# A hybrid decoder layer on one core: x enters transposed, split without the token norm, the norm's factor applied to the projections' results

## The reference

```
h    = x * rsqrt(mean(x*x) + 1e-6) * norm_g          # token norm: one factor per token, one gain per feature
proj = h @ w_in                                       # 1024 x 4608, split in ten parts
oa   = rmsnorm(retention(qa, ka, va), ret_norm_g)     # 4 heads of 128, chunks of 128 tokens, a state
ob   = rglru(conv4(xb))                               # 512 channels, gates by sigmoid, a scan over tokens
oc   = attention(rmsnorm(qc), rmsnorm(kc), vc)        # window of 128, ALiBi, sinks, 4 heads on 2 kv heads
y    = x + concat(oa*silu(ga), ob*silu(gb), oc*silu(gc)) @ w_out
```

## Time and profile before

| | |
|---|---|
| median of three runs | 729.69 us |
| the profiled execution: its span, which is its own time as shown | 730.9 us |
| TensorE matmuls busy | 718.1 us, 98% |
| VectorE, ACT, POOL busy | 296.6, 268.6, 100.3 us |
| mean granted clock of TensorE | 0.981 |
| loaded and stored | 50 MB, 68 GB/s in the mean |

### The profile page before, as it was taken

One profiled execution on the slowest core, in us unless ns is written; L12 is line 12 of the kernel. 1 busy time (PEld: TensorE's weight loads), 2 busy tenths in 40 slices (PEclk: granted clock), 3 DMA queues, 4 the chain that ended last, 5 costly groups with the idle time before them and its releaser, 6 DMA issues. The chain is left out here.

```text
span 730.9 us, 11478 instructions
## 1 busy us (share of the span) xinstructions
PE 718.1 (98%) x4486; PEld 662.0 (91%) x4486; DVE 296.6 (41%) x693; ACT 268.6 (37%) x693; POOL 100.3 (14%) x228
## 2 busy tenths in 40 slices
PE   6999999999999999999999999999999999999998
PEld 4999989999999899999999998999989988888884
DVE  5824421232424213788632386317733362211102
ACT  5822422231323222678923464326453351000000
POOL 2201600353525000000002211122100000000000
PEclk9999989999999899999999999999999999999999
DMA  7511042103030211110131011031011351222111
GB/s 247 188 59 58 1 158 74 59 2 119 1 119 1 90 34 54 58 39 21 59 125 55 18 59 30 1 95 49 12 30 58 144 202 31 84 87 86 58 37 36
DMA packets 22887, 50.04 MB, mean 68 GB/s; under 512 B 1645, under 2 KB 15341, under 8 KB 20498
## 3 DMA queue, kind: packets, MB, share of 16 engines
q1 hardware_dynamic: 22834, 49.31, 19.8%
HBM read 42.22 MB, written 9.12 MB: 70 GB/s over the span
## 5 line engine op out<-in xcount | busy, mean ns | idle before, releaser
L377 PE MATMUL proj<-big 128*128 128x352 f32 (+1 forms) x960 | 311.3, 324 | 0.6 <-ACT big L786 0.6
L378 PE MATMUL proj<-big 128*128 128x352 f32 (+1 forms) x960 | 298.4, 311 | 0.0
L379 PE MATMUL proj<-big 128*128 128x352 f32 (+1 forms) x960 | 298.4, 311 | 0.0
L377 PEld LDWEIGHTS proj<-big 128*128 128x128 f32 x960 | 185.8, 193 | 9.9 <-issue 6.7
L378 PEld LDWEIGHTS proj<-big 128*128 128x128 f32 x960 | 185.6, 193 | 0.7
L379 PEld LDWEIGHTS proj<-big 128*128 128x128 f32 x960 | 185.6, 193 | 0.0
L1108 DVE TENSOR_TENSOR big<-raw,big 128x512 fp32r<-128x512 f32 x72 | 49.5, 694 | 62.7 <-ACT big L772 62.7
L1515 POOL TENSOR_SCALAR stat<-stat 128x1 f32<-128x1 f32 (+3 forms) x77 | 15.6, 203 | 321.4 <-ACT junk L900 197.3
L379 PE MATMUL branch<-big,m_parts 128*128 128x512 f32 x144 | 56.0, 389 | 0.0
L378 PE MATMUL branch<-big,m_parts 128*128 128x512 f32 x144 | 56.0, 389 | 0.0
L377 PE MATMUL branch<-big,m_parts 128*128 128x512 f32 x144 | 56.0, 389 | 0.0
(11 more groups left out here) (213 smaller groups left out, 940.5 us busy)
## 6 DMA issues: line engine op xcount, KB each, us to landing
raw<-w_units SPq DMA_DIRECT2D x18, 1024.0 KB, 4.8
mixed<-x_prompt SPq DMA_DIRECT2D x8, 512.0 KB, 5.2
x_res<-x_prompt SPq DMA_DIRECT2D x8, 512.0 KB, 4.2
out_y_prompt<-y_out SPq DMA_DIRECT2D x8, 512.0 KB, 2.9
raw<-w_out SPq DMA_DIRECT2D x6, 512.0 KB, 3.9
y_out<-w_out SPq DMA_DIRECT2D x6, 512.0 KB, 4.5
s<-state_ret SPq DMA_DIRECT2D x4, 512.0 KB, 4.2
out_s_ret<-s SPq DMA_DIRECT2D x4, 512.0 KB, 3.8
```

The lines of the kernel that those rows point to most:

```text
L377: pe.matmul(out, a_lo, b_hi, start=first, stop=False)
L378: pe.matmul(out, a_hi, b_lo, start=False, stop=False)
L379: return pe.matmul(out, a_hi, b_hi, start=False, stop=last)
```

## The change

- **x transposed.** The host also hands over x_T, x with features on partitions, in three chunks of 352 tokens. Each chunk is loaded in four pieces: chunk 0 on ACT's queue, the others on SyncE's (SP), behind four pieces of the first unit's weights. ACT's x_hi is a copy with scale norm_g (a column of the parameters), VectorE's x_lo is x * norm_g - h_hi. The loads of x by tile, x_stat, x_scale, turn_x and the spread of norm_g are gone, and so is turn_states (the states come transposed).
- **First unit.** Unit 0 is now qk 0. It runs by chunks: for each chunk, both halves of 128 features over eight blocks k, in two banks; six banks are used in turn. v 0 becomes unit 1.
- **The token factor.** ACT squares each chunk in two halves, VectorE adds them; in unit 1 nine matmuls with ones sum over features (token_squares), VectorE and POOL make the factor per token (rcol) and epsilon terms (ecol), nine diagonal matrices and nine matmuls spread it over partitions (rb).
- **Where it is applied.** v: in the evacuation. qk: in the retention's mask and k_dec; the norms of the retention's output, of qC and kC take a scaled epsilon in its place. xb: a multiply at the head of conv. gB, gC: plain evacuation, then one multiply (gate_row) and one Silu (gate_silu) for each row of 1056 columns. gA: multiply in the bank on VectorE, Silu in the bank on ACT, product into mixed on VectorE (ga_mix), which frees the bank.
- **Buffers.** ig of the RG-LRU has one buffer; the attention's bias is loaded in two parts; tail_rows lies in pT; the load of s0 of head 0 waits for rb.

The core of the diff:

```diff
-UNITS = [("v", 0), ("qk", 0), ("v", 1), ...
+UNITS = [("qk", 0), ("v", 0), ("v", 1), ...
+    if kind == "gA":
+        return "mix_g", 6 * i + j + 1
...
+            def first_unit():
+                for c in range(3):
+                    banks = [proj_bank(2 * c), proj_bank(2 * c + 1)]
+                    cols = slice(c * CH, (c + 1) * CH)
+                    if c == 2:
+                        pe.wait_ge(S_["act_freed"], 2)
+                    for k in range(KD):
+                        pe.wait_ge(S_["h_hi_set"], KD * c + k + 1)
+                        pe.wait_ge(S_["h_lo_set"], KD * c + k + 1)
+                        if c == 0 and k % 2 == 0:
+                            pe.wait_ge(S_["w_hi_set"], k // 2 + 1)
+                            pe.wait_ge(S_["w_lo_set"], k // 2 + 1)
...
+            def token_squares():
+                pe.wait_ge(S_["ones_set"], 1)
+                pe.wait_ge(S_["sq_added"], 6)
+                for t in range(NT + 1):
+                    mm = pe.matmul(bb[4][0:tile_rows(t), 2 * t:2 * t + 2], sqs[:, chunk_cols(t)], ones[:, 0:2],
+                                   start=True, stop=True)
+            def spread_scale():
+                for t in range(NT + 1):
+                    if t % 4 == 0:
+                        pe.wait_ge(S_["diag_set"], min(t + 4, NT + 1))
+                    mm = pe.matmul(bb[(2, 3, 4)[t // 4]][:, (t % 4) * P:(t % 4) * P + n], ones[:],
+                                   dgs[:, t * P:t * P + n], start=True, stop=True)
...
+                if (u, s) == (1, 0):
+                    token_squares()
+                if (u, s) == (1, 3):
+                    spread_scale()
...
+            def x_square(c, half):
+                if c + half > 0:
+                    act.wait_ge(S_["sq_added"], 2 * c + half)
+                act.activation(sqt[:].rearrange("p (k n) -> p k n", k=4), xs[c][:, 4 * half:4 * half + 4, :],
+                               ACT.Square).then_inc(S_["sq_set"], 1)
...
+                if q == 3 and f >= 1:
+                    act.wait_ge(S_["lru_set"], f)
...
+            for q in range(4):
+                act.dma_start(xs[0][:, 2 * q:2 * q + 2, :], x_piece(0, q)).then_inc(S_[f"x_in{q}"], 16)
+            act.wait_ge(S_["par_in"], 16)
+            for p in range(PIECES):
+                w_hi(0, p)
+                x_hi(0, 2 * p)
+                x_hi(0, 2 * p + 1)
+            for k in range(KD):
+                x_hi(1, k)
+            x_square(0, 0)
+            x_square(0, 1)
+            evacuate(0, 0)
+            evacuate(0, 1)
+            for k in range(KD):
+                x_hi(2, k)
+            x_square(1, 0)
+            x_square(1, 1)
+            evacuate(0, 2)
+            evacuate(0, 3)
+            for p in range(PIECES):
+                w_hi(1, p)
+            x_square(2, 0)
+            x_square(2, 1)
+            evacuate(0, 4)
+            evacuate(0, 5)
...
+            def square_sum(c):
+                total = sqs[:, c * CH:(c + 1) * CH]
+                for half in range(2):
+                    dve.wait_ge(S_["sq_set"], 2 * c + half + 1)
+                    link(dve.tensor_tensor(sqt[:, 0:2 * CH], sqt[:, 0:2 * CH], sqt[:, 2 * CH:4 * CH], ALU.add))
+                    if half == 0:
+                        dve.tensor_tensor(total, sqt[:, 0:CH], sqt[:, CH:2 * CH], ALU.add).then_inc(
+                            S_["sq_added"], 1)
+                        continue
+                    link(dve.tensor_tensor(sqt[:, 0:CH], sqt[:, 0:CH], sqt[:, CH:2 * CH], ALU.add))
+                    dve.wait_ge(S_["sq_added"], 2 * c + 1)
+                    dve.tensor_tensor(total, total, sqt[:, 0:CH], ALU.add).then_inc(S_["sq_added"], 1)
...
+            def gate_row(u, mt):
+                dve.wait_ge(S_["act_freed"], freed(u, 3 * mt + 2)[1])
+                dve.tensor_tensor(mixed[:, row, :], mixed[:, row, :], rb[:], ALU.mult).then_inc(S_["row_set"], 1)
...
+                link(dve.tensor_tensor(xb[:, i, 3:3 + SEQ], xb[:, i, 3:3 + SEQ], rb[:, 0:SEQ], ALU.mult))
...
+            for p in range(PIECES):
+                w_low(0, p)
+                x_lo(0, 2 * p)
+                x_lo(0, 2 * p + 1)
+            for k in range(KD):
+                x_lo(1, k)
+            square_sum(0)
+            for k in range(KD):
+                x_lo(2, k)
+            square_sum(1)
+            for p in range(PIECES):
+                w_low(1, p)
+            square_sum(2)
```

More of the change, by code:

```diff
@@ L391, in group_half @@
             def group_half(u, j, half):
                 g = FIRST_GROUP[u] + j
-                bank = pb[g % 3]
+                bank = proj_bank(g)
                 if half == 0:
                     if j == 0:
[L396 to L404, removed]
+                        pe.wait_ge(S_["w_lo_set"], PIECES * (u + 1))
+                        pe.wait_ge(S_["w_hi_set"], PIECES * (u + 1))
+                    name, n = freed(*GROUPS[g - 3])
+                    pe.wait_ge(S_[name], n)
@@ L422, in group_half @@
                     mm.then_inc(S_["proj_done"], 1)
[L424 to L433, removed]
-                        mm = pe.transpose(bank[:, i * P:i * P + n], x_in[t % XS][0:n, k * P:(k + 1) * P],
-                                          ident[0:n, 0:n])
-                    mm.then_inc(S_["x_turned_b" if q else "x_turned_a"], 1)
             def ret_one(m):
@@ L766, in w_hi @@
             def w_hi(u, piece):
-                act.wait_ge(S_["raw_in"], 16 * (u + 1))
+                if u == 0:
+                    act.wait_ge(S_[f"w0_in{piece}"], 16)
+                else:
+                    act.wait_ge(S_["raw_in"], 16 * u)
                 if u >= 2:
@@ new lines, in spread_copy, with gate_silu @@
+            def spread_copy():
+                for i in range(3):
+                    n = 4 * P if i < 2 else NS
+                    act.wait_ge(S_["spread"], i + 1)
+                    act.activation(rb[:, i * 4 * P:i * 4 * P + n], bb[2 + i][:, 0:n], ACT.Copy).then_inc(
+                        S_["rb_set"], 1)
+            def gate_silu(r):
+                act.wait_ge(S_["row_set"], r + 1)
+                row = 4 + r
+                act.activation(mixed[:, row, :], mixed[:, row, :], ACT.Silu).then_inc(S_["gate_set"], 1)
@@ L794, in fold_copy, with ga_gate @@
+            def ga_gate(e):
+                act.wait_ge(S_["ga_set"], e + 1)
+                bank = proj_bank(FIRST_GROUP[16] + e)
+                act.activation(bank[:, 0:CH], bank[:, 0:CH], ACT.Silu).then_inc(S_["ga_silu"], 1)
             def fold_copy(u):
@@ L808, in evacuate @@
                 act.wait_ge(S_["proj_done"], g + 1)
[L809 to L810 removed]
+                bank = proj_bank(g)
+                mt, c = (j % 2, j // 2) if u == 0 else (j // 3, j % 3)
                 cols = slice(c * CH, (c + 1) * CH)
@@ L813, in evacuate @@
                     n = tile_rows(j)
-                    ins = act.activation(v_tok[0:n, i, j, :], bank[0:n, 0:UNIT], ACT.Copy)
+                    if i == 0 and j == 0:
+                        act.wait_ge(S_["rcol_set"], 3)
+                    ins = act.activation(v_tok[0:n, i, j, :], bank[0:n, 0:UNIT], ACT.Copy,
+                                         scale=rcol[0:n, j:j + 1])
                 elif kind == "qk":
@@ L1141, in ret_mask, with ga_mix @@
+            def ga_mix(e):
+                bank = proj_bank(FIRST_GROUP[16] + e)
+                dve.wait_ge(S_["ga_silu"], e + 1)
+                row, cols = e // 3, slice((e % 3) * CH, (e % 3 + 1) * CH)
+                dve.tensor_tensor(mixed[:, row, cols], mixed[:, row, cols], bank[:, 0:CH], ALU.mult).then_inc(
+                    S_["mix_g"], 1)
             def ret_mask(m):
```

382 lines of the change are left out of this document (183 added, 199 removed).

## The result

The changed kernel takes 739.23 us (median of 4 runs, 736.38 to 740.77) where the kernel before takes 729.76 on the same chip (4 runs, 728.22 to 732.28): ratio 1.0122, interval 1.0091 to 1.0154. It is slower by more than the range on record (725.0 to 736.5) allowed.

The account below looks back on a forecast made before the run. TensorE, with matmuls busy for 98% of the span, was taken as the bound. The terms -0.6 (unit 2's start), +1.5 (RG-LRU), +0.3 and +0.3 gave +1.5 us, 731.2; the forecast was centred at 731.4, range 725.0 to 736.5.

Parts of the forecast that it names:

- The relay of squares: Unit 1: ACT's squares and VectorE's adds alternate without overlap, ending at 37.3; TensorE waits 3.4 us at token_squares.
- Rival A: At token_squares: the relay is shorter and the clock holds, giving 724.3 us, or 727.7 with only the clock holding; chance 0.28.
- Start after: Head: with x and weights in pieces on two queues, the first projection matmul starts at 6.2 us, against 13.66 before.
- rival D: Head: the DMA pieces land 1 us later than taken, moving VectorE's chain and unit 1, +1 us; no chance of its own.
- 1.0 wait: Start of unit 1: TensorE, ready at 31.5, waits 1.0 us for VectorE's low parts, which end at 32.4.
- +3.5: Unit 1: the wait and tiny matmuls at token_squares lower TensorE's clock, costing 3.5 us, bounds 0 and 5.
- RG-LRU stage: Units 8 to 11: VectorE's added work delays the low parts of unit 11's weights; TensorE waits 1.5 us, bounds 0 and 4.
- conv 3 makes it 2.9: RG-LRU: VectorE's scan 1, pushed 1.3 us by conv 2, is 2.9 us late after conv 3.
- Rival B: RG-LRU: unit 11's wait is followed by a late evacuation of group (10, 5); +4 in place of 1.5; chance 0.17.
- Starts elsewhere unchanged: Sign for the profile after: apart from the listed changes in head, unit 2 and unit 11, starts stay as they were.
- Against the median this gives 731.2: Last step: the summed +1.5 us is set against the profiled span of 730.9, taken as 1.2 above the median of 729.69.
- two terms of +0.3: One for gate_row in unit 6, one for gA's path through VectorE, ACT and VectorE; +0.3 us each.

Follow-up runs that it names:

- squares_late: The changed kernel with token_squares and the spread of the factor two slots later in unit 1: 733.58 us, ratio 1.0052 to the kernel before.
- start_early: The changed kernel with the params transfer behind the first piece of weights and ScalarE's table load ahead of its wait: 737.93 us, ratio 1.0095.
- silu_late: The changed kernel with the first two whole-row Silus of gC moved behind the evacuations of (11, 0) and (11, 1): 735.38 us, ratio 1.0067.
- before_shift_64: The kernel before with 64 unused bytes ahead of m_parts, nothing else: 734.31 us, ratio 1.0056.
- shift_704: The changed kernel with 704 unused bytes ahead of m_parts: 734.18 us, ratio 1.0052 to the kernel before.
- shift_64: The changed kernel with 64 unused bytes ahead of m_parts, nothing else: 738.01 us, ratio 1.0099 to the kernel before.

## Why the prediction was wrong

The direction (slower, at 0.42 the likeliest of the three) was right. The size, +1.5 against +9.5, was not. The steps that failed are the RG-LRU term, the output phase that was put at nothing, and the way from the profile to the median. By its own steps:

- **"The relay of squares"**: right. "3.4 wait" at token_squares was measured as 3.4 (TensorE resumed at 40.17 and not at 37.3, since all of it lay later), and squares_late, which gains 4.2 in the trace, shows that the wait and its low clock are real. Rival A, in which this wait falls away, didn't come about; its own 724.3 lay outside the range of 725.0 to 736.5 that was to cover it.
- **"Start after ... TensorE starts at 6.2"**: wrong, 9.9. Two terms: the weight piece was taken to land at 4.3 by the earlier trace rows, and landed at 6.5 behind params (rival D, with 2.2 in place of 1); and ScalarE's table load (1.28), which the kernel before ran at 0.71, ahead of its first data, was left out. start_early undid both and got 7.26.
- **"1.0 wait" at unit 1 and "+3.5" of low clock**: 0 and about 1.2 in this execution (69.1 less 9.9, 47.7, 2.5, 3.4, 2.2 and 2.2). TensorE came later, so there was no wait. The 3.5 was not too much in itself: with longer stretches the same wait cost 2.7 and 3.6 in the other kernels. With the start these cancel: 3.7 - 1.0 - 2.3 = +0.4, so unit 2 was forecast at 68.7 and started at 69.1. That the sum came out is luck.
- **"RG-LRU stage" (+1.5)**: the first failing term, measured 4.9, above its upper bound of 4. The count of VectorE's delay was sound: "conv 3 makes it 2.9" answers to a square root 2.8 later against TensorE's gates. Its exit was wrong. The text led the delay only down VectorE's own order, to the low parts of unit 11, and set 4.7 against a margin of 3.3; they ended at 357.9, 3.2 later than before and not 4.7, and no run shows TensorE waiting for them at unit 11. The delay left through ScalarE: the late square root stands ahead of a sigmoid that frees a bank of the gates, and there the margin was nothing. Of the wait of 3.4 there, 2.8 is that delay and 0.6 ScalarE's longer row with the whole-row Silu that was called "hidden"; the stretch of low clock behind it cost 1.7 more. silu_late took away 2.4 of wait and the stretch, 3.9 together. Rival B had the size (4 and a low stretch) with another bank. By the prediction's own sign ("unit 11 starts without a wait") this step is wrong.
- **"Starts elsewhere unchanged"**: the second failing term, 3.9 in the output phase against 0. The diff leaves that phase's matmuls as they are; the new and dropped tiles moved m_parts by 1344 bytes. before_shift_64 puts the same loss into the kernel before with no other change, and shift_704 takes it out of the changed one.
- **"Against the median this gives 731.2"**: the third failing term, 4.2 us. The profiled execution of before had a low clock for that kernel (0.981, where its other runs had 0.981 to 0.991) and lay 2.9 above its median. The text compared a span (730.9) with times of runs (729.69) and so saw 1.2 of it. The changed kernel's profiled execution lay 1.2 below its median; two of its three other runs had a lower clock (0.979). It had caught the shortest stretch at token_squares of the seven kernels with that wait, and each 3.4 us more of low clock costs up to 1.7. Which stretches the unprofiled runs had isn't recorded, so that this is what lowered their clock is not shown.

Measured by the traces: -0.2 to unit 2, -0.8 to unit 10, +4.9, then -2.4 where two low stretches are absent, +3.9: +5.4, against 5.3. The other 4.2 us are the third term. The two terms of +0.3 are too small to be told from the steps of the low clock.

## What to carry to other kernels

Count the order of every in-order engine to each thing that it frees, PSUM banks above all: a delay on one engine has to be followed through every engine that waits for it, and not only down its own order; here VectorE's 2.8 us came out on TensorE by way of ScalarE. When a change adds or removes an SBUF tile, compare the addresses of the tiles that TensorE's later phases read; 704 unused bytes took 3.9 us off the output phase here, about as much as a wait of 3 us with its low clock. And compare a profiled execution with the runs by its mean granted clock before a median is forecast from it, a span with spans and a time with times. An early start is worth only what the next chained work lets through: 1.2 of 2.6 us here, at unit 1.

## What the hardware showed unexpectedly

- Matmuls of 512 columns in three passes with 128x128 stationary operands in fp32r were 0.2267 us apart with m_parts at remainder 128 by 256, 0.2333 at 192 and 0.2324 at 0, with nothing waited for. The output phase with its 576 of them took 145.1 us, 148.9 and 148.3. Why is not shown.
- In the changed kernel ScalarE's first table load came after its first wait had ended (6.58, when the weights landed) and not while it waited; in the kernel before it ran at 0.71, ahead of the wait. It took 1.28 us, and the next operation began 0.01 behind it. The Trainium skill (ScalarE: Activation LUTs, "What ACT_TABLE_LOAD costs") gives the same 1283 ns, and a drain of about 1380 ns besides for each switch to another set of functions; behind this load no such drain shows, nor behind the one at 350.03 in unit 10.
- Behind 3.2 us of idle TensorE and matmuls of 2 columns the clock fell at 42.2; with the same small matmuls and no idle time it did not (squares_late). The stretch behind the same wait was 3.4, 6.8 or 10.2 us long in seven kernels, and began within the wait in some of them (39.1 in shift_64). In the kernel before, a stretch began at 95.3 as 16 matmuls of 4 columns ended, with TensorE not idle.
- A transfer of 25 KB in rows of 200 bytes, issued 0.44 ahead of the first 256 KB of weights, went with a landing of those 1.3 us later than when it was issued behind them; 0.44 of that is their own later issue.
